# Rotary embedding: exchanging head halves with DMAs between SBUF tiles instead of a permutation matmul

## What is computed

```python
u = h @ w_in                      # a_b, a_c, a_x, q, k, v, c_in
q = apply_rope(q, cos, sin)       # 8 heads of 64 features; k alike
#   x1, x2 = split(x, 2, axis=-1)
#   concatenate([x1*cos - x2*sin, x2*cos + x1*sin])
o = diff_attention(q, k, v, lam)  # causal, two softmaxes per head pair
y_b = rmsnorm(o, g) * (1 - lam_init)
c = causal_depthwise_conv(glu(c_in), conf_dw_w)   # 31 taps
y_c = silu(layernorm(c))
y_a = a_b * causal_depthwise_conv(a_c * a_x, short_conv_w)
x = x + concatenate([y_a, y_b, y_c]) @ w_out
```

## Time and profile before

| | |
|---|---|
| median of 3 runs | 2474.83 us |
| the profiled execution's own time | 2473.95 us |
| its span, first to last instruction | 2472.3 us |
| TensorE matmul, weight load busy | 98%, 81% |
| VectorE, ScalarE, GpSimd busy | 41%, 38%, 48% |
| chain of work that ended last: TensorE | 91% |
| mean granted TensorE clock | 0.993 |

### The profile page before, as it was taken

The page is one execution under the profiler, slowest core; times in us unless marked ns, Lnnn a source line. Parts: engine busy times, 40 slices in busy tenths (PEclk is TensorE's granted clock), DMA queues, the critical chain, the costliest instruction groups (busy, mean ns, idle before and its releaser), DMA issues.

```text
span 2472.3 us, 35533 instructions
## 1 busy us (share of the span) xinstructions
PE 2425.7 (98%) x14295; PEld 2004.9 (81%) x14295; DVE 1007.0 (41%) x2261; ACT 935.4 (38%) x1435; POOL 1182.7 (48%) x1566
## 2 busy tenths in 40 slices
PE   8999999999999999999999999999999999999998
PEld 6888888888788888888888888877868887888887
DVE  7974211124874211123867774224345333211113
ACT  5553222224563322224544453235553344322221
POOL 5125655654115565655533233443326645655563
PEclk9999999999999999999999999999999999999999
DMA  5532223224632223224211111232213322223222
GB/s 177 139 103 86 102 88 109 99 77 130 164 103 86 103 81 115 85 85 141 94 58 53 53 52 53 81 133 86 69 58 128 116 96 79 96 86 110 103 80 83
DMA packets 42403, 237.17 MB, mean 96 GB/s; under 512 B 4736, under 2 KB 7936, under 8 KB 19712
## 3 DMA queue, kind: packets, MB, share of 16 engines
q1 hardware_dynamic: 39936, 218.13, 25.0%
q0 software_dynamic: 2304, 16.78, 3.3%
HBM read 213.92 MB, written 4.19 MB: 88 GB/s over the span
## 4 chain that ended last, share of the span: by engine, by line
PE 91%; DVE 4%; POOL 2%; issue 1%; ACT 1%; DMA 1%; SPq 0%; DVEq 0%; POOLq 0%; ACTq 0%
PE PB L1886 75%; PE PB L1888 4%; POOL WL L3028 1%; PE PB L1898 1%; PE PB L1923 1%; PE PB L2136 1%; PE PB L2117 1%; DVE cc L2614 1%; PE PB L1970 1%; PE PB L1987 1%; PE PB L2124 1%; DMA WR<-in_w_in 1%; PE PB L2148 1%; PE PB L2164 1%; PE PB L2087 0%
## 5 line engine op out<-in xcount | busy, mean ns | idle before, releaser
L3028 POOL TENSOR_TENSOR WL<-WR,WH 128x256 fp32r<-128x256 f32 (+1 forms) x1444 | 1055.0, 767 | 753.6 <-ACT WH L2183 753.6
L1886 PE MATMUL PB<-HH,WH 128*128 128x512 f32 x1992 | 795.0, 399 | 11.0 <-ACT HH L2198 10.5
L1886 PE MATMUL PB<-HL,WH 128*128 128x512 f32 x1992 | 779.4, 391 | 0.9 <-DVE HL L2506 0.9
L1886 PE MATMUL PB<-HH,WL 128*128 128x512 f32 x1992 | 516.5, 396 | 0.8 <-DMA WL<-WR 0.8
L2183 ACT ACTIVATE WH<-WR 128x2048 fp32r<-128x2048 f32 (+1 forms) x209 | 371.9, 1779 | 245.9 <-PE PB L1886 238.2
L1886 PEld LDWEIGHTS PB<-HH,WH 128*128 128x128 f32 x1992 | 375.8, 189 | 101.2 <-issue 13.7
L1886 PEld LDWEIGHTS PB<-HL,WH 128*128 128x128 f32 x1992 | 375.8, 189 | 76.9 <-issue 1.7
L1886 PEld LDWEIGHTS PB<-HH,WL 128*128 128x128 f32 x1992 | 366.4, 188 | 75.3 <-issue 2.0
L1886 PE MATMUL PB<-BL,WH 128*128 128x512 f32 (+1 forms) x859 | 331.6, 387 | 0.6 <-DVE BL L2515 0.6
L1886 PE MATMUL PB<-BH,WH 128*128 128x512 f32 (+1 forms) x795 | 307.9, 388 | 1.3 <-ACT BH L2218 1.3
L1886 PE MATMUL PB<-BH,WL 128*128 128x512 f32 (+1 forms) x795 | 195.0, 389 | 1.5 <-POOL WL L3028 1.5
(11 more groups left out here) (363 smaller groups left out, 2678.4 us busy)
## 6 DMA issues: line engine op xcount, KB each, us to landing
WR<-in_w_gu SPq DMA_DIRECT2D x66, 1024.0 KB, 4.7
WR<-in_w_dn SPq DMA_DIRECT2D x48, 704.0 KB, 4.0
WR<-in_w_in SPq DMA_DIRECT2D x22, 1024.0 KB, 4.8
WL<-WR POOLq DMA_DIRECT2D x16, 1024.0 KB, 6.9
WR<-in_qkv SPq DMA_DIRECT2D x12, 1024.0 KB, 4.7
WR<-in_w_out SPq DMA_DIRECT2D x8, 1024.0 KB, 4.7
WR<-in_qk SPq DMA_DIRECT2D x8, 1024.0 KB, 4.8
WR<-in_gb SPq DMA_DIRECT2D x4, 1024.0 KB, 4.7
```

What stands on the lines that cost most here:

```text
L1886: ins = pe.matmul(out[:, 0:n], wt[:, k * cols + j * P:k * cols + (j + 1) * P], x[:, k, t0:t0 + n], start=first, stop=last)
L3028: g.tensor_tensor(m.WL[u % 2][:, part], m.WR[u % 2][:, part], f32(m.WH[u % 2][:, part]), ALU.subtract).then_inc(sems["wlo"], 1)
```

## The change

The permutation product is gone, with its matrix in the constants. In its place a step swap follows each qkin: SP issues four DMAs, each of which copies 32 partitions x 512 of qr (64 KB) to the neighbouring 32 partitions of one of three new tiles qs. VectorE multiplies and adds from qs. The step rot is set two evictions after its qkin instead of one. The table ROUGH takes 1.4 us of VectorE for a rot and none of TensorE, and the clock takes a swap as there 9.0 us after its qkin. The rotation's multiplication by sin no longer waits for GpSimd's product, only the addition does.

```diff
-    "rot": [("T", 0.9, 0), ("V", 1.5, 0)], ...
+    "rot": [("V", 1.4, 0)], ...
...
-        def rotate(name, c, q):
-            room = fbank.take()
-            t = Tile(room, room.after)
-            pe("rot", l, name, c, tile=t, q=q.i, tok=at("qkin", l, name, c), after=f)
-            room.free(at("rots", l, name, c))
+        def rotate(name, c, q, x):
+            step("rot", l, name, c, q=q.i, x=x.i, swapped=swapped[name, c], after=f)
             q.free(at("rot", l, name, c))
-            turned[name, c] = True
+            x.free(at("rot", l, name, c))
...
-                    if waiting:
-                        rotate(*waiting)
-                    waiting = name, c, q
+                    if len(waiting) == 2:
+                        rotate(*waiting.pop(0))
+                    x = qss.take()
+                    swaps[x.i] += 1
+                    swapped[name, c] = f"swap{x.i}", 64 * swaps[x.i]
+                    step("swap", l, name, c, q=q.i, x=x.i, after=x.after)
+                    clock.when[swapped[name, c]] = clock.when[at("qkin", l, name, c)] + 9.0
+                    waiting.append((name, c, q, x))
...
-        elif kind == "rot":
-            te.all(w["tile"].after)
-            te.wait_ge(*at("qkin", *key))
-            pe.matmul(PB[w["tile"].b][:], m.CON[:, C_SWAP:C_SWAP + P], m.qr[w["q"]][:], start=True, stop=True).then_inc(tile, 1)
...
-            q, dst = m.qr[w["q"]], (m.Q if name == "q" else m.K)
-            ve.wait_ge(*w["tile"].done)
+            x, dst = m.qs[w["x"]], (m.Q if name == "q" else m.K)
+            ve.wait_ge(*w["swapped"])
             ve.wait_ge(*at("rsin", l))
+            v.tensor_tensor(x[:], x[:], m.RSIN[:], ALU.mult).then_inc(sems["rots"], 1)
+            ve.wait_ge(*at("rots", *key))
             ve.wait_ge(*at("rotc", *key))
-            v.tensor_tensor(q[:], PB[w["tile"].b][:], m.RSIN[:], ALU.mult).then_inc(sems["rots"], 1)
-            ve.wait_ge(*at("rots", *key))
-            v.tensor_tensor(dst[:, c, :], dst[:, c, :], q[:], ALU.add).then_inc(sems["rot"], 1)
+            v.tensor_tensor(dst[:, c, :], dst[:, c, :], x[:], ALU.add).then_inc(sems["rot"], 1)
...
+        elif kind == "swap":
+            l, name, c = key
+            se.wait_ge(*at("qkin", *key))
+            se.all(w["after"])
+            for x in range(4):
+                q.dma_start(m.qs[w["x"]][32 * x:32 * x + 32, :], m.qr[w["q"]][32 * (x ^ 1):32 * (x ^ 1) + 32, :]).then_inc(sems[f"swap{w['x']}"], 16)
```

More of the change, by code:

```diff
@@ L61 @@
 NVEC = _n
-C_ID, C_ONE, C_INVF, C_SGN, C_SWAP, C_CAUS, C_INCL, C_LEV, C_EYE, C_RST = 0, 128, 256, 257, 264, 392, 904, 1032, 1192, 1224
-NCON = 1736
+C_ID, C_ONE, C_INVF, C_SGN, C_CAUS, C_INCL, C_LEV, C_EYE, C_RST = 0, 128, 256, 257, 264, 776, 904, 1064, 1096
+NCON = 1608
 def constants():
@@ L73, in constants @@
     c[:, C_ONE:C_ONE + P] = 1.0
-    c[:, C_SWAP:C_SWAP + P] = (r ^ 32) == k
     c[:, C_CAUS + 384:C_CAUS + S] = np.where(k <= r, 0.0, NEG)
@@ L149, in memory @@
              ("cp0", [P, 30 + S]), ("cp1", [P, 30 + S]), ("cc0", [P, S]), ("cc1", [P, S]), ("ct", [P, S]), ("sm", [P, 96]), ("rcos", [P, S])]
-    names += [(f"pa{i}{n}", [P, S]) for i in range(3) for n in range(2)]
+    names += [(f"pa{i}{n}", [P, S]) for i in range(3) for n in range(2)] + [(f"qs{i}", [P, S]) for i in range(3)]
     m.qr0, m.qr1, m.Q, m.K, m.VT, m.cx, cp0, cp1, cc0, cc1, m.ct, m.sm, rcos, *pa = run(g1, b0, *names)
-    pa += run(tail1, end, ("pa30", [P, S]), ("pa31", [P, S]))
+    pa[6:6] = run(tail1, end, ("pa30", [P, S]), ("pa31", [P, S]))
+    m.qs = pa[8:11]
     m.RCOS, m.RSIN, m.R2 = rcos, m.ct, rcos
@@ L241 @@
     "lnsum": (), "lnsub": ("V:lnsub",), "lnmul": ("V:lnmul",), "lnact": ("A:lnact",),
-    "scaled": ("V:rcos", "V:rsin"), "r2": ("A:r2",), "qkin": ("A:qkin",), "rot": ("G:rotc", "V:rots", "V:rot"), "vin": ("A:vin",),
+    "scaled": ("V:rcos", "V:rsin"), "r2": ("A:r2",), "qkin": ("A:qkin",), "swap": (), "rot": ("G:rotc", "V:rots", "V:rot"), "vin": ("A:vin",),
     "sh1": ("V:sh1",), "sh2": ("V:sh2",), "sh3": ("V:sh3",), "sh4": ("V:sh4a", "V:sh4"),
@@ L873, in ffn @@
         return toks, fo2
-    rope = []
+    rope, swaps = [], [0, 0, 0]
     def block1(l, fo, then):
@@ L885, in block1 @@
         qrs = Ring([Room(i) for i in range(4)], clock)
-        for q in qrs.rooms:
+        qss, swapped = Ring([Room(i) for i in range(3)], clock), {}
+        for q in qrs.rooms + qss.rooms:
             q.free(*f)
@@ L942, in conv_taps @@
                 yield
-        turned = {}
-        def rotate(name, c, q):
-            room = fbank.take()
-            t = Tile(room, room.after)
-            pe("rot", l, name, c, tile=t, q=q.i, tok=at("qkin", l, name, c), after=f)
-            room.free(at("rots", l, name, c))
+        def rotate(name, c, q, x):
+            step("rot", l, name, c, q=q.i, x=x.i, swapped=swapped[name, c], after=f)
             q.free(at("rot", l, name, c))
-            turned[name, c] = True
+            x.free(at("rot", l, name, c))
         v_in = set()
         def heads_in(p):
-            waiting = None
+            waiting = []
             for name in "qk":
@@ L3069, in sync_program @@
     q.dma_start(m.VECS[:, 0:first_vecs], d["vecs"][:, 0:first_vecs]).then_inc(sems["vec0"], 16)
-    q.dma_start(m.CON[:, C_INVF:C_SWAP], d["con"][:, C_INVF:C_SWAP]).then_inc(sems["rope"], 16)
+    q.dma_start(m.CON[:, C_INVF:C_CAUS], d["con"][:, C_INVF:C_CAUS]).then_inc(sems["rope"], 16)
     q.dma_start(m.POSI[:], d["pos"]).then_inc(sems["pos"], 16)
@@ L3077, in sync_program @@
     q.dma_start(m.VECS[:, first_vecs:NVEC], d["vecs"][:, first_vecs:NVEC]).then_inc(sems["vec1"], 16)
-    q.dma_start(m.CON[:, C_SWAP:NCON], d["con"][:, C_SWAP:NCON]).then_inc(sems["con1"], 16)
+    q.dma_start(m.CON[:, C_CAUS:NCON], d["con"][:, C_CAUS:NCON]).then_inc(sems["con1"], 16)
     stored = 0
@@ L3113, in build @@
         o = order(m)
-        names = ["tile", "vchain", "vec0", "vec1", "con0", "con1", "rope", "pos", "w0", "w1", "wlo0", "wlo1", "memt", "away", "out"]
+        names = ["swap0", "swap1", "swap2", "tile", "vchain", "vec0", "vec1", "con0", "con1", "rope", "pos", "w0", "w1", "wlo0", "wlo1", "memt", "away", "out"]
         names += [f"x{c}" for c in range(DC)] + [f"bt{i}{j}" for i in range(2) for j in range(2)]
```

## The result

The changed kernel takes **2511.2 us** (median of 4 runs, 2508.6 to 2511.8), the kernel before beside it 2476.7: ratio 1.0139, 95% interval 1.0125 to 1.0154, so some 34 us slower. The forecast was 2485.2 with a range of 2468 to 2497. The sign was right, the size was not, and the range missed by 14 us.

A forecast was written before the change was run, and what follows sets the result against it. TensorE, 91% of the chain, was taken as the bound. The terms -13.9 + 1.0 + 4.3 + 16.6 + 2.4 gave +10.4 us on 2473.95, and with 0.9 for the median 2485.2 us, range 2468 to 2497.

The forecast's parts named there:

- The products, -13.9: TensorE, both layers: removing 16 permutation products of 0.87 us each saves their whole length, 13.9 us.
- WL later, +4.3: TensorE's waits for WL by accumulating DMA, both layers: WL comes no earlier while TensorE arrives sooner; +4.3 us (1 to 8).
- The pause in layer 0, +16.6: Layer 0's output projection, chunk 6: TensorE idles for the filter's norm, moved later in the list; +16.6 us (8 to 22).
- the clock, +2.4: After layer 0's pause: TensorE's matmuls run at the lower clock for a while; +2.4 us (0 to 2.4).
- Layer 1 "without such a gap": Layer 1: no TensorE pause like layer 0's at the filter's norm.
- The exchanges, +1.0: Swap DMAs on SP land about 6 us after issue; lateness costs nothing in layer 0, +1.0 us in layer 1.
- its cover is V's product: Layer 0's scores: they come only after V, by which time K is rotated, so late swaps cost TensorE nothing.
- (A): The forecast itself: pause in layer 0 of 12 to 20 us, net +3 to +17 us; chance 0.58.
- (D): Rival: swaps land much later than 6 us, holding VectorE 5 to 10 us more, four times; +18 to +30; chance 0.10.
- (C): Rival: faster, no pause in layer 0 and swaps hidden; -9 to -13 us, about 2464; chance 0.12.
- the rule weighed in the forecast: VectorE's sin multiplication, now from two SBUF inputs, contends with GpSimd; counted as nothing, at most 5.6 us.

The follow-up runs named there:

- run 3: Kernel before with each permutation product cut to one column and VectorE multiplying the unexchanged copy; 2477.1 us, ratio 0.9996.
- run 1: Changed kernel, order of all engines kept, with the 64 exchange DMAs left out; 2500.9 us, ratio 1.0088.
- runs 6: Changed kernel with its DMAs, but the planner counting a rotation as before (0.9 us of TensorE, 1.5 of VectorE); 2498.2 us, ratio 1.0080.
- run 7: Changed kernel with the planner's rotation costs of before and the 64 exchange DMAs left out; 2480.8 us, ratio 1.0011.
- run 5: Kernel before with only the filter's lead in layer 0 set from 1.0 to 0.6, so its norm comes late; 2505.8 us, ratio 1.0116.
- run 2: Changed kernel with the same 64 DMAs issued from ScalarE's queue right behind its copy, instead of from SP; 2513.8 us, ratio 1.0145.

## Why the prediction was right and wrong

- **The products, -13.9: failed.** This is the first step that fell. The length of a product on TensorE's sequence was read rightly, but worth was set equal to length. Cut to one column in the kernel before (10.4 us less for TensorE) they give 1.0 us (from 4.5 gained to 2.5 lost by the interval of run 3). The sentence behind it, that TensorE is 91% of the chain, is true of the whole kernel and does not carry that: the first eight products, four a layer, stand where the chain runs through GpSimd, DMAs and VectorE, so that a lighter TensorE only waits longer there (2.4, 1.2, 1.4 and 2.1 us in run 3, for 0.4, 0.8, 0.8 and 0.4 before). The window of 60 to 80 us had the sign of it, VectorE busy for 19.35 of 20 us, and I did not weigh it. With this term alone put at -1 the forecast's sum would have been about +23, or 2498.
- **WL later, +4.3: right in size.** 5.0 + 2.1 us of wait, against 0.4 + 0 and 0.8 before, is +5.9. The reason was mostly wrong: the DMA takes 12.8 us without any exchange beside it (run 1), and 13.2 with and 11.8 without in runs 6 and 7, so the exchanges make 0.1 to 1.4 us of it.
- **The pause in layer 0, +16.6 and the clock, +2.4: right.** In the changed kernel 26.2 us pass from where TensorE ran dry (175.4) to chunk 6; 6.4 of them are its own work at full clock by the forecast's count, and 1.8 more are lost behind at half clock: 21.6 for 19.0. Alone, in run 5, it cost 25.9. The shorter difference of runs 1 and 7, 14.3, has a wait of 5.8 us left in the better order.
- **Layer 1 "without such a gap": failed.** It has one of 5.7 us for BH and one of 3.0 for V's copy. It rested on the statement made with the change that in layer 1 the filter's norm still ends before the output projection starts, and that is true of one of its two chunks only. In us of the layer's weight products ahead of it in the list, the norm's last step for chunk 6 moved from 100.2 to 117.6, and that for chunk 7 from 103.4 to 122.1, behind the output projection's first product at 120.3. The wait of 5.7 us is the one for chunk 7: TensorE had done the products of chunks 0, 2, 3 and 6 by 777, and chunk 7's BH was ready at 783.2. The order alone costs 8.6 us in layer 1 (run 1 against run 7).
- **The exchanges, +1.0: failed.** Each figure lay inside or near its bounds, but "its cover is V's product" did not hold. Landing: 8.9 us for Q's and 7.3 for the last of K's (bounds 2.7 to 8.6, I took 6). Issue: 0.95 us each, eight in 7.63 and K's four in 3.8 (I took 0.5). K's turn on SP: 67.35, for 64.4, as the load waits for a WL DMA that is itself 3 us longer. The three add up to K at 78.6 in place of 70, just past V, and VectorE, with no time to spare, hands its 10 us on to everything behind it. Worth 10 us in the order of the change, 17 in a better one.
- **The rivals.** What happened is (A) and a part of (D) together, and I had priced them as alternatives: landings of 9 us, and VectorE held four times, as (D) had it, but for 10 us in the two waits of layer 0 and 13 in the two of layer 1. (C) fell with the first row of the pause. The half clock, which the sum has at one place, comes at six: behind the waits of 5.0 and 3.4 us and from 188 on through that of 6.1 in layer 0, behind those of 3.2, 3.0 and 5.7 in layer 1.

Summed by runs: products about -1 (run 3), order 23 to 24 (run 1 less run 3), DMAs 10 to 13 (the change less run 1), together 32 to 36, for 34 measured.

## What to carry to other kernels

A product taken from the engine that is 91% of the chain is worth its length only if it stands on the chain in its own stretch, and if the others have room behind it. Ask the trace for the chain of that stretch, and time the kernel with the product left out before replacing it. Here this one run would have shown that there was nothing to win. Where a planner sets the order, a changed cost moves steps far from the edit; look for the last step of each moved chain, not for its first, in every layer. And a small transfer that is needed soon must not stand behind a large one on an in-order queue. It landed in 2 us at an idle queue and in 9 right behind a load, but what cost more here was that it also waited for whatever the load waited for, 12 us for K.

## What the runs showed of the hardware

- Issuing a DMA of 32 partitions x 2 KB between two SBUF tiles cost the issuing engine 0.6 to 1.1 us (run 2: four in 2.44 to 4.37 us on ScalarE, 64 in 50 us; the changed kernel: eight in 7.63 and 7.33 us on SP in layer 0), where a 128 x 2 KB load of X cost SP 0.5.
- An accumulating DMA of a megabyte took longer when it started together with a load of the same size: 11.8 to 13.8 us in eight traces with the two starts 0.1 us apart, 8.6 to 10.4 in six with the load 1.1 to 2.4 us ahead. No run varied this alone.
- The lower clock came often, and after short waits: behind the wait of 2.4 us in run 3 the granted clock was 0.50 from 66 to 68 us, while behind that of 2.1 us at 657 in the changed kernel it stayed at 1.00. In the forecast only the longest pause was charged with it.
- VectorE's addition of two SBUF tiles took 3.71 us once in the changed kernel, at 658.1 (0.69 elsewhere, but for one of 1.69), while GpSimd's two multiplications by cos ran from 658.4 to 661.3; before it had one of 3.20. The Trainium skill, page SBUF — State Buffer, section Who interferes with whom, names this contention, and these rows agree with it. It was there before and after alike, and the multiplication, which now reads two SBUF tiles instead of PSUM, kept its median of 0.68 us (1.36 once): the rule weighed in the forecast cost next to nothing here. In run 3, where it met GpSimd's multiplications instead of the addition, it took 3.93 us once.
